# A transformer block pair on one core: product in PSUM, finer waits, and another order of ScalarE's attention work

## The reference

```
first block, each layer:
  h = rms_norm(x);  z = h @ w_in          -> qa, ka, va, qi, ki, wi, cq, ckv, kr, ga, gb
  y_a = attention of 8 heads over the 128 keys that the index scores choose, with a bias
  y_b = latent attention of 8 heads (keys and values from ckv), masked by chunks of 64
  merged = sigmoid(ga + b) * (y_a @ w_proj_a) + sigmoid(gb + b) * (y_b @ w_proj_b)
  x = x + merged @ w_out
  u = causal_dwconv(rms_norm(x) @ w_up)   # 3 taps over the tokens, 2 x 2816 columns
  x = x + (silu(u_gate) * u_val) @ w_down
second block:
  dilated attention (kind "A"), compressed, selected ("sel") and window ("win") attention
  h = h + mix @ w_out;  h = h + (silu(hn @ w_gate) * (hn @ w_up)) @ w_down;  rms_norm(h)
```

## Time and profile before

| | |
|---|---|
| three runs, us | 2392.25 median (2392.19 to 2394.22) |
| profiled execution, own time | 2393.93 us |
| its span, first to last instruction | 2392.1 us |
| TensorE matmuls busy | 2335.4 us, 98% |
| VectorE, ScalarE, GpSimd busy | 52%, 26%, 66% |
| granted TensorE clock, mean | 0.997 of full speed |

### The profile page before, as it was taken

The page is one execution under the profiler, slowest core; times in us unless marked ns, Lnnn a source line. Parts: engine busy times, 40 slices in busy tenths (PEclk is TensorE's granted clock), DMA queues, the critical chain, the costliest instruction groups (busy, mean ns, idle before and its releaser), DMA issues.

```text
span 2392.1 us, 34530 instructions
## 1 busy us (share of the span) xinstructions
PE 2335.4 (98%) x11106; PEld 1759.3 (74%) x11106; DVE 1242.4 (52%) x2116; ACT 614.4 (26%) x1349; POOL 1589.5 (66%) x818
## 2 busy tenths in 40 slices
PE   7999999999999999999999999999999999999997
PEld 5665578878888776655788788887787567887886
DVE  5677653366416536775543665165545755440442
ACT  4334620231101233336202311012322753000001
POOL 5564367777777775543687778777766437777775
PEclk9999999999999999999999999999999999999999
DMA  6122022223223222220233223322362002322222
GB/s 204 63 79 99 18 71 89 96 88 95 90 96 96 88 91 69 79 99 19 63 96 97 88 88 97 97 89 96 125 220 97 19 10 88 97 89 96 91 93 88
DMA packets 61586, 212.65 MB, mean 89 GB/s; under 512 B 6344, under 2 KB 6728, under 8 KB 61328
## 3 DMA queue, kind: packets, MB, share of 16 engines
q1 hardware_dynamic: 54368, 194.38, 25.5%
q10 hardware_dynamic: 7088, 16.58, 2.1%
HBM read 208.78 MB, written 10.01 MB: 91 GB/s over the span
## 4 chain that ended last, share of the span: by engine, by line
PE 89%; DVE 3%; ACT 3%; issue 2%; DVEq 2%; DMA 0%; POOL 0%; ACTq 0%; SPq 0%; POOLq 0%
PE out_tile L509 77%; PE turned L655 3%; PE stat L672 2%; ACT sq L1141 1%; PE out_tile L1013 1%; PE out_tile L729 1%; PE out_tile L827 1%; PE out_tile L832 1%; ACT arena L1151 1%; PE out_tile L837 1%; DVEq L1459 1%; PE turned L632 1%; DMA x<-x_t 0%; PE stat L509 0%; PE out_tile L847 0%
## 5 line engine op out<-in xcount | busy, mean ns | idle before, releaser
L509 PE MATMUL out_tile<-arena_r,w_hi 128*128 128x512 f32 x5240 | 1648.2, 395 | 0.0
L509 PEld LDWEIGHTS out_tile<-arena_r,w_hi 128*128 128x128 f32 x5240 | 984.5, 188 | 239.6 <-issue 1.9
L509 PE MATMUL out_tile<-arena_r,w_lo 128*128 128x512 f32 x2620 | 1046.7, 400 | 15.3 <-POOL w_lo L1914 3.6
L1908 POOL TENSOR_TENSOR w_hi<-weight_ring,cst 128x1024 fp32r<-128x1024 f32 (+1 forms) x348 | 659.4, 1895 | 539.4 <-PE out_tile L509 475.4
L1914 POOL TENSOR_TENSOR w_lo<-weight_ring,w_hi 128x1024 fp32r<-128x1024 f32 (+1 forms) x348 | 850.6, 2444 | 26.8
L509 PEld LDWEIGHTS out_tile<-arena_r,w_lo 128*128 128x128 f32 x2620 | 492.1, 188 | 164.9 <-issue 32.4
L1437 DVE TENSOR_TENSOR x<-out_tile,x 128x512 f32<-128x512 f32 x72 | 49.8, 692 | 339.1 <-PE out_tile L509 339.0
L1258 ACT ACTIVATE work<-out_tile,p 128x512 f32<-128x512 f32 x88 | 65.8, 773 | 375.0 <-PE out_tile L509 263.1
L1372 DVE CAST arena_r<-work 128x512 f32 (+2 forms) x84 | 137.0, 1631 | 13.0 <-issue 11.8
L1374 DVE TENSOR_TENSOR arena_r<-work,arena_r 128x512 f32 (+2 forms) x84 | 135.6, 1614 | 13.4 <-issue 12.1
L1698 DVE SCALAR_TENSOR_TENSOR work<-out_tile,p,work 128x511 f32<-128x511 f32 x88 | 65.6, 745 | 136.7 <-ACT work L1258 136.7
(11 more groups left out here) (213 smaller groups left out, 1835.8 us busy)
## 6 DMA issues: line engine op xcount, KB each, us to landing
weight_ring<-stream SPq DMA_DIRECT2D x356, 512.0 KB, 3.5
arena<-bias_rows ACTq DMA_DIRECT2D x4, 2048.0 KB, 12.1
bias_rows<-bias_kept ACTq DMA_DIRECT2D x2, 2556.0 KB, 22.0
bias_rows<-bias_kept SPq DMA_DIRECT2D x1, 2556.0 KB, 14.3
x<-x_t SPq DMA_DIRECT2D x4, 512.0 KB, 9.6
arena<-w ACTq DMA_DIRECT2D x1, 2048.0 KB, 8.4
out_t<-arena SPq DMA_DIRECT2D x8, 256.0 KB, 2.2
cst<-consts SPq DMA_DIRECT2D x1, 576.0 KB, 14.5
```

Of the source, the lines that this page charges most:

```text
L509: ins = pe.matmul(out, l, r, start=start and n == 0, stop=stop and n == 2, **kw)
L1908: pool.tensor_tensor(blocks_of(w_hi[:, s % SPLIT, :], used), blocks_of(ring[:, s, :], used), cols(cst, C_ONE).unsqueeze(1).to_broadcast([P ...
```

## The change

Five edits. (1) ScalarE's attention loop goes by pairs: both copies of pair i-3, then both exponentials of pair i. (2) In the merge stage tile pb 0 is freed by a ScalarE copy into the bank stat[1], and VectorE multiplies from there. (3) In the up stages the product of value and gate half is kept in PSUM, in stat[0] or turn[0]; the second tap of even tiles writes there, with a copy of the first two columns, and the split reads from there. Section B does the same with its product. (4) TensorE waits for each bank of an interleaved pair by itself, ahead of the first matmul into it, where it waited for both; in section B a wait for all tiles of the stage before is dropped. (5) In the last residual, the square of chunk 6 is added before the residual of chunk 7.

```diff
--- before.py
+++ after.py
@@ -138,7 +138,7 @@
         t += attention_tiles(ITEMS_1[2 * n:2 * n + 2]) + [(("vb", n), "a")]
     t += attention_tiles(ITEMS_1[2 * QB:])
     for j in range(DC):
-        projections, gates = [(("pb", j), "v"), (("pa", j), "v")], [(("gb", j), "a"), (("ga", j), "a")]
+        projections, gates = [(("pb", j), "v" if j else "a"), (("pa", j), "v")], [(("gb", j), "a"), (("ga", j), "a")]
         t += gates + projections if j else projections + gates
     t += [(("out", j), "v") for j in range(DC)]
     for part, (first, n) in enumerate(HALVES):
@@ -317,6 +317,9 @@
         qi, ki = chunks(32, 4), chunks(36, 1)
         misc, kr_all = chunks(37, 1), chunks(38, 1)
         rows_both = arena_r[:, 39, :]
+
+        def product(n):
+            return turn[0] if n else stat[0]
         cq, ckv = parts(40, 43), parts(46, 48)
         maskb = arena[:, 43, :]
         sel = chunks(50, 3)
@@ -874,9 +877,10 @@
                     with pe.Fori(1 - part, n // 2) as i:
                         for s in (0, 2):
 
-                            pe.wait_ge(A.taken["v"], L * A.count["v"] + i * 4 + (v0 + s - 3))
                             for k in range(DC):
                                 for e in range(2):
+                                    if k == 0:
+                                        pe.wait_ge(A.taken["v"], L * A.count["v"] + i * 4 + (v0 + s + e - 4))
                                     w = weight(i, 4)
                                     ins = matmul(psum[(n0 + s + e) % 4][:, :], w, h_ffn(k), start=(k == 0),
                                                  stop=(k == DC - 1))
@@ -1028,7 +1032,6 @@
             for part, (first, n) in enumerate(HALVES):
                 n0 = B.tile_no(("gate", first))
                 v0, a0, at = B.release[n0 + 1][1] - 1, B.release[n0][1] - 1, state["block"]
-                pe.wait_ge(B.taken["v"], v0)
                 if part == 0:
                     linear_pair((("gate", 0), ("upp", 0)), h_ffn, DC, ready=LAYERS * 5 * DC + 2 * DC,
                                 beside={2: lambda: norm_sum(LAYERS, FFN)}, used=True)
@@ -1038,9 +1041,11 @@
                     for s in (0, 2):
 
                         pe.wait_ge(B.taken["a"], i * 2 + (a0 + s // 2 - 1))
-                        pe.wait_ge(B.taken["v"], i * 2 + (v0 + s // 2 - 1))
+                        pe.wait_ge(B.taken["v"], i * 2 + (v0 + s - 3))
                         for k in range(DC):
                             for e in range(2):
+                                if (k, e) == (0, 1):
+                                    pe.wait_ge(B.taken["v"], i * 2 + (v0 + s // 2 - 1))
                                 w = weight(i, 4)
                                 ins = matmul(psum[(n0 + s + e) % 4][:, :], w, h_ffn(k), start=(k == 0),
                                              stop=(k == DC - 1))
@@ -1132,24 +1137,34 @@
             def attention(sec, L, turned, width, beside={}):
 
                 items = sec.items
-                for n in range(len(items) + 2 * LAG_TURN):
-                    if n in beside:
-                        beside[n]()
-                    if n < len(items):
-                        sec.wait_taken(act, L, ("score",) + items[n])
-                        w = width(items[n])
-                        act.activation(prob(n, w), prob(n, w), ACT.Exp, scale=-1.0,
-                                       bias=negmax[:, n % 8:n % 8 + 1], accum_out=rsum[:, n % 8:n % 8 + 1])\
-                           .then_inc(sec.exp_done, 1)
-                    if n >= 2 * LAG_TURN:
-                        m = n - 2 * LAG_TURN
-                        kind, h, b = items[m]
-                        if m >= 2 * SLOTS:
-                            act.wait_ge(sec.pv_done, L * sec.pairs + m // 2 - SLOTS + 1)
-                        act.wait_ge(sec.turn_done, L * len(items) + m + 1)
-                        w = (b + 1) * P
-                        act.activation(turned[:, m % (2 * SLOTS), 0:w], turn[m % 2][:, 0:w], ACT.Copy)\
-                           .then_inc(sec.turn_taken, 1)
+
+                def take_turned(m):
+
+                    kind, h, b = items[m]
+                    if m >= 2 * SLOTS:
+                        act.wait_ge(sec.pv_done, L * sec.pairs + m // 2 - SLOTS + 1)
+                    act.wait_ge(sec.turn_done, L * len(items) + m + 1)
+                    w = (b + 1) * P
+                    act.activation(turned[:, m % (2 * SLOTS), 0:w], turn[m % 2][:, 0:w], ACT.Copy)\
+                       .then_inc(sec.turn_taken, 1)
+
+                def exponential(n):
+
+                    sec.wait_taken(act, L, ("score",) + items[n])
+                    w = width(items[n])
+                    act.activation(prob(n, w), prob(n, w), ACT.Exp, scale=-1.0,
+                                   bias=negmax[:, n % 8:n % 8 + 1], accum_out=rsum[:, n % 8:n % 8 + 1])\
+                       .then_inc(sec.exp_done, 1)
+
+                for i in range(0, len(items) + 2 * LAG_TURN, 2):
+                    for n in (i, i + 1):
+                        if n in beside:
+                            beside[n]()
+                        if n >= 2 * LAG_TURN:
+                            take_turned(n - 2 * LAG_TURN)
+                    for n in (i, i + 1):
+                        if n < len(items):
+                            exponential(n)
 
             act.wait_ge(load_p1, 16)
             def first_upper(k):
@@ -1231,6 +1246,8 @@
                 attention(A, L, turned1, lambda item: (item[2] + 1) * P, {2 * b + 2: take_values(b) for b in range(QB)})
                 load_table(ACT.Sigmoid)
                 norm_upper(L * 3 * DC + DC, h_ffn)
+                A.wait_done(act, L, ("pb", 0))
+                act.activation(stat[1][:, :], psum[A.tile_no(("pb", 0)) % 4][:, :], ACT.Copy).then_inc(A.taken["a"], 1)
                 for j in range(DC):
                     for g, name in ((1, "gb"), (0, "ga")):
                         A.wait_done(act, L, (name, j))
@@ -1433,11 +1450,14 @@
             def residual(sec, L, key, norm=None, raw=None):
 
                 for j in range(DC + 1):
+                    early = norm and not raw and j == DC - 1
+                    if early:
+                        add_square(norm[0], norm[1], j - 1)
                     if j < DC:
                         took(dve.tensor_tensor(x[:, j, :], tile(sec, L, key(j))[:, :], x[:, j, :], ALU.add), sec)
                     if raw and j >= 1:
                         raw_lower(raw[0], j - 1, raw[1])
-                    if norm and j >= 1:
+                    if norm and j >= 1 and not early:
                         add_square(norm[0], norm[1], j - 1)
 
             def scale_index_queries(L, scale):
@@ -1666,8 +1686,11 @@
                 norm_input(L * 3 * DC + DC, lambda k: p1col(L, PC_MIX + k), stat[0][:, :], h_ffn)
                 for j in range(DC):
                     A.wait_taken(dve, L, ("gb", j))
-                    took(dve.tensor_tensor(work[:, 5, :], tile(A, L, ("pb", j))[:, :], work[:, 2 * (j % 2) + 1, :],
-                                           ALU.mult), A)
+                    if j == 0:
+                        dve.tensor_tensor(work[:, 5, :], stat[1][:, :], work[:, 1, :], ALU.mult)
+                    else:
+                        took(dve.tensor_tensor(work[:, 5, :], tile(A, L, ("pb", j))[:, :], work[:, 2 * (j % 2) + 1, :],
+                                               ALU.mult), A)
                     A.wait_taken(dve, L, ("ga", j))
                     took(dve.tensor_tensor(work[:, 4, :], tile(A, L, ("pa", j))[:, :], work[:, 2 * (j % 2), :],
                                            ALU.mult), A)
@@ -1685,7 +1708,7 @@
                     with dve.Fori(0, n // 2) as i:
                         def gated(s):
                             dve.wait_ge(silu_done, L * FC + i * 2 + (first + s + 1))
-                            t = work[:, 2 * s:2 * s + 1, :]
+                            t = product(s)[:, :].unsqueeze(1)
                             dve.tensor_tensor(t, t, work[:, 4 + s:5 + s, :], ALU.mult)
                             dve.drain()
                             split(t, [arena_r[:, bass.ds(i * 2 + (h + s), 1), :] for h in hid]).then_inc(hid_done, 1)
@@ -1699,7 +1722,11 @@
                                                      scalar=p1[:, bass.ds(c + 1, 1)], in1=work[:, s, 1:S],
                                                      op0=ALU.mult, op1=ALU.add)
                             dve.drain()
-                            took(dve.scalar_tensor_tensor(out=work[:, s, 2:S], in0=ps[:, 0:S - 2],
+                            t = work[:, s, :]
+                            if s % 2 == 0:
+                                t = product(s // 2)
+                                dve.tensor_copy(t[:, 0:2], work[:, s, 0:2])
+                            took(dve.scalar_tensor_tensor(out=t[:, 2:S], in0=ps[:, 0:S - 2],
```

(4 more changed lines are left out.)

## The result

The changed kernel takes 2350.67 us (median of 5 executions, 2350.01 to 2352.11), the kernel before beside it 2392.25 (5 executions, 2391.44 to 2394.22). The ratio is 0.9827, 95% interval 0.9814 to 0.9841: faster by 1.7%. Three executions with a far lower granted clock are left out of every median, range and ratio here: 2547.53 us (0.851) of the kernel before, 7371.51 (0.302) of before_again, 2726.58 (0.781) of product_in_sbuf. The forecast was 2355.6 with a range from 2351.0, so the sign was right and the gain larger than forecast: 41.6 us where 36.6 were expected, and 0.33 us outside the range.

The account below looks back on a forecast made before the run. TensorE, busy 98% of the span, was taken as the bound. 26.0 + 2.7 + 1.2 + 3.5 + 2.4 + 0.8 = 36.6 us off the median 2392.25 gave 2355.6, own range 2351 to 2361, 8 in 10 2351 to 2369.

Parts of the forecast that it names:

- Attention, 26.0: Attention stages: with ScalarE's copies ahead of the exponentials, TensorE's transposes stop waiting, gaining 26.0 us against 13.5 listed.
- (a): Rival: attention returns only the listed 13.5 us, other waits on VectorE or GpSimd taking over; 2368.1 us, chance 0.20.
- (d): Rival: the new attention order does nothing, transposes waiting for the same copies; all 26.0 missing, 2381.6 us, chance 0.07.
- (e): Rival: late exponentials delay transposes three pairs on, which delay copies again; slower, 2400 at 0.4 us a pair, chance 0.03.
- the prediction's own sign of being wrong: Attention: transposes waiting for VectorE's or GpSimd's scaled pieces instead of ScalarE's copy would show the prediction wrong.
- Merge, 2.7: Merge stage: ScalarE's early copy of pb 0 removes TensorE's wait for VectorE's multiply, 2.7 us.
- Up stage, start, 1.2: First up loop pass: separate waits let three matmuls run earlier, less 0.12 for the two-column copy, 1.2 us in two layers.
- Up stage, end, 3.5: Down stage's wait for the last hidden chunk: product in PSUM shortens VectorE's three steps to 0.7 us each, 3.5 us.
- Rival (c): End of up stage: product in PSUM is no faster, VectorE's chain ends as late; + 3.5, 2359.1 us, chance 0.04.
- Second section, 2.4, and tail, 0.8: Dropping the second section's wait for all eight tiles gains 2.4 us; adding chunk 6's square earlier in the tail, 0.8.
- Added waits, 0: TensorE's 60 added waits, for tiles freed long before, cost 0, with 6 us as the bound.
- the 5.0 us of the scattered waits: Attention: 12 of the 34 listed transpose waits lie in other places, 3.8 us, taken as 5.0 with restarts.

Follow-up runs that it names:

- before_again: The kernel before, unchanged, timed and profiled a second time: 2390.99 us, ratio 0.9999.
- product_in_sbuf: The changed kernel with the gated product back in SBUF and no copy of two columns: 2357.97 us, ratio 0.9864 to the kernel before.
- refined: The changed kernel with VectorE's last split per attention stage moved later, the two-column copy behind the bank's release, and an early last table load: 2351.35 us.
- order_alone: The kernel before with only ScalarE's new attention loop order: 2364.18 us, ratio 0.9886.
- all_but_order: The changed kernel with ScalarE's old attention loop order: 2379.71 us, ratio 0.9955 to the kernel before.
- coarse_waits: The changed kernel with TensorE's old waits in the up and gate stages: 2355.21 us, ratio 0.9852 to the kernel before.

## Why the prediction was right, and where it was not

- **Attention, 26.0.** Measured 26.8 in the changed kernel, 26.5 alone, 27.1 when taken away. The step that mattered, counting what a group of transposes lost and not what the list called a wait, was right: a period of four pairs became 0.97 us shorter, 0.94 were forecast. But the layers gave 0.8 more each and the second section 0.9 less. In the ledger of the layers a group of four transposes gave 0.86 us where 0.68 was counted, since its first transpose had started 0.2 late too, without a wait in the list, and a group of six 0.37 for 0.29; in the second section a period gave the 0.98 that its groups of four and two add up to. Where that section's 0.9 were lost wasn't followed beyond its end. No wait for a scaled piece came up within a stage, so neither (a) nor (d) nor (e) came. At the very end of each stage one did, the prediction's own sign of being wrong, at 1.3 us in all: GpSimd's scaling stood there behind VectorE's split of a finished group, and moving the split gave 0.6, 0.6 and 0.25 us (refined). The prediction didn't look at the ends.
- **Merge, 2.7.** 2.9.
- **Up stage, start, 1.2.** 2.2, the term most off. Each wait gave 0.76 where 0.70 - 0.12 was forecast: the copy sits in a gap and costs 0.04. The remaining 0.35 us a layer come from the normalised input just ahead, for which the sum has no term: VectorE stood 0.54 us before one instruction there in the kernel before and 0.18 in the changed one. They are missing in order_alone and there in all_but_order, product_in_sbuf and coarse_waits, so they go with an edit of VectorE's program outside of the product, or only with how that program lies; that wasn't parted.
- **Up stage, end, 3.5.** 3.6, and 3.6 when undone alone. Rival (c) is out: in PSUM each of the three steps takes 0.7 us. The rule of the Trainium skill ("VectorE: DVE Perf Modes", section "Why PSUM operands drop a tier") holds for the fastest cast, 0.43 us from SBUF against 0.69, but not for the mean of 1396 ns that the kernel gets there. The prediction took that mean as a price of its own; the trace shows it to be two, 0.43 us where GpSimd is idle and the rest of a GpSimd instruction more where it isn't.
- **Second section, 2.4, and tail, 0.8.** 2.5 and 0.8. The second half of the norm's sum was ready.
- **Added waits, 0.** Right; 560 more cost nothing within the up loops.
- **The step that failed.** The mechanisms held; sizes of the sum did not. The term most off is that of the first loop pass, "Gain 2 x (0.70 - 0.12) = 1.2 us; the rest of this wait stays", which measured 2.2. With attention at 26.8 for 26.0 and 0.3 in the small terms the edits brought 38.7 us for 36.6. The other 2.9 of the measured 41.6 lie outside of every edit, and there the prediction put nothing, without a reason: it held the rest of the profiled execution for fixed, while two executions of the same program differ by 4.9 us there. The range failed with it: "Its own range is 2351 to 2361: 4 to 5 us on either side, since the 5.0 us of the scattered waits and the restart of 0.26 at each stall could both be off by half" takes in only the errors of its own terms. Either part alone, put right, would have left 2350.67 inside the range. It was 0.33 us out, and the changed kernel's second median, 2352.74, is in; the two differ by 2.1, so on which side of the bound the first one fell was chance, the 2.1 us missing at the edits were not.

## What to carry to other kernels

Where two engines hand over in a fixed order, put the instruction that releases the busiest engine ahead of those that only feed a later step, and price the gain by the length of the groups against that of undisturbed ones: the list of waits showed half of it. A short instruction may be free if it fills the gap between two dependent ones, and cost more than twice its length a line further on. Where VectorE's and GpSimd's work meet in SBUF, look at what GpSimd does at the start of each slow instruction before taking the mean for a price. Before a single trace is taken as the reference for a sum, compare two of the same kernel by the start of the same matmul: what differs there is the width that no term explains.

## What was not expected of the hardware

- An unchanged program has spans of 2392.1 and 2387.2 us. Of the 4.9 us, 3.0 are two stretches of 3.41 us each in which TensorE's granted clock is at half (1.2 GHz); TensorE reads as 100% busy in them. All begin 0.5 to 1.3 us after the start of the last small matmul of the rotary keys, in 7 and 3 of 12 traces, and cost 1.5 to 1.6 us each.
- VectorE's multiplies, casts and subtractions of 128x512 from SBUF to SBUF took 0.43 to 2.73 us in the kernel before. The long ones all began while a GpSimd instruction ran and ended 0.28 to 0.55 us after it. With a source in PSUM they took 0.68 to 0.70 us beside GpSimd too. The steady price was worth more than the low one.
- 560 more waits on TensorE whose condition already held changed the pace of the up loops by no more than 0.02 us.
